# One inference step of a two-layer hybrid backbone on one core: out_proj's last token block is finished in the stage that follows

## What is computed

```python
h = rms_norm(x, g_pre1) * (1 + scale1) + shift1
y, ctx_out = token_mixers(h, *mix_params, ctx=ctx)
x = x + gate1 * rms_norm(y, g_post1)
h = rms_norm(x, g_pre2) * (1 + scale2) + shift2
x = x + gate2 * rms_norm(ffn(h), g_post2)
```

## Time and profile before

| | |
|---|---|
| median of three runs | 2105.94 us (2105.35 to 2110.06) |
| the profiled execution | 2105.66 us, span 2103.9 us |
| mean granted TensorE clock | 0.965 of full |
| PE busy | 1936.0 us, 92% of the span |
| DVE busy | 1296.7 us, 62% |
| ACT busy | 1046.1 us, 50% |
| POOL busy | 95.1 us, 5% |
| DMA | 302.25 MB, mean 144 GB/s, best of 40 slices 410 GB/s |
| loads `side<-ffn_w_gate`, issue to landing | 3.9 us, median |

### The profile page before, as it was taken

The page is one execution under the profiler, slowest core; times in us unless marked ns, Lnnn a source line. Parts: engine busy times, 40 slices in busy tenths (PEclk is TensorE's granted clock), DMA queues, the critical chain, the costliest instruction groups (busy, mean ns, idle before and its releaser), DMA issues. The chain is left out here.

```text
span 2103.9 us, 32195 instructions
## 1 busy us (share of the span) xinstructions
PE 1936.0 (92%) x11352; PEld 1618.4 (77%) x11352; DVE 1296.7 (62%) x1958; ACT 1046.1 (50%) x1689; POOL 95.1 (5%) x62
## 2 busy tenths in 40 slices
PE   4998899897999999997998999877999999999993
PEld 2996555597998998986986555876888888888883
DVE  3725656573323323356627565645888888888886
ACT  4214344444111112144235254535888888888884
POOL 0320000000000000001300000002000000000001
PEclk9999999898999999998999999888999999999997
DMA  6205512202223213212225601139967291827464
GB/s 252 95 26 200 198 41 101 100 1 71 76 81 96 70 63 90 80 41 90 70 81 213 266 1 40 62 136 393 410 250 282 87 345 50 343 94 275 173 245 160
DMA packets 130339, 302.25 MB, mean 144 GB/s; under 512 B 17984, under 2 KB 63936, under 8 KB 127296
## 3 DMA queue, kind: packets, MB, share of 16 engines
q1 hardware_dynamic: 124240, 279.10, 36.3%
q10 hardware_dynamic: 3120, 11.28, 1.4%
q0 software_dynamic: 2880, 10.49, 1.3%
HBM read 369.21 MB, written 28.61 MB: 189 GB/s over the span
## 5 line engine op out<-in xcount | busy, mean ns | idle before, releaser
L2208 DVE TENSOR_TENSOR ex_wl<-ex_raw,ex_wh 128x1024 fp32r<-128x1024 f32 x351 | 419.4, 1222 | 28.4 <-ACT ex_wh L2086 17.2
L2086 ACT ACTIVATE ex_wh<-ex_raw 128x1024 fp32r<-128x1024 f32 x351 | 368.2, 1060 | 74.7 <-PE psum L2143 46.2
L2491 PE MATMUL psum<-norm_out,ex_w_hi 128*128 128x320 f32 x1408 | 264.6, 309 | 4.3 <-PEq L1582 4.3
L2143 PE MATMUL psum<-ex_wh,ex_he_hi 128*128 128x512 f32 (+1 forms) x624 | 242.6, 389 | 12.7 <-DVE ex_wl L2208 12.7
L2143 PE MATMUL psum<-ex_wl,ex_he_hi 128*128 128x512 f32 (+1 forms) x624 | 233.5, 374 | 0.0
L2143 PE MATMUL psum<-ex_wh,ex_he_lo 128*128 128x512 f32 (+1 forms) x624 | 233.0, 373 | 0.0
L2491 PEld LDWEIGHTS psum<-norm_out,ex_w_hi 128*128 128x128 f32 x1408 | 222.2, 188 | 4.8 <-issue 4.6
L2358 DVE TENSOR_TENSOR ex_w_lo<-side,ex_w_hi 128x1024 fp32r<-128x1024 f32 (+1 forms) x82 | 82.6, 1014 | 169.4 <-ACT ex_w_hi L2354 169.2
L2491 PE MATMUL psum<-norm_out,ex_w_lo 128*128 128x320 f32 x704 | 160.3, 308 | 0.0
L2143 PEld LDWEIGHTS psum<-ex_wh,ex_he_hi 128*128 128x128 f32 x624 | 118.2, 189 | 35.3 <-issue 14.2
L2143 PEld LDWEIGHTS psum<-ex_wh,ex_he_lo 128*128 128x128 f32 x624 | 118.3, 190 | 22.0 <-issue 2.9
(11 more groups left out here) (401 smaller groups left out, 3819.9 us busy)
## 6 DMA issues: line engine op xcount, KB each, us to landing
ex_raw<-moe_gate_up SPq DMA_DIRECT2D x236, 512.0 KB
ex_raw<-moe_w_down SPq DMA_DIRECT2D x143, 512.0 KB
x<-moe_gate_up SPq DMA_DIRECT2D x70, 512.0 KB
wmod_ssd<-w_mod SPq DMA_DIRECT2D x56, 512.0 KB, 5.7
wmod_at<-w_mod SPq DMA_DIRECT2D x24, 512.0 KB, 4.2
side<-ffn_w_gate SPq DMA_DIRECT2D x22, 512.0 KB, 3.9
side<-ffn_w_up SPq DMA_DIRECT2D x22, 512.0 KB, 3.9
mx_qkv_room<-w_in SPq DMA_DIRECT2D x10, 1024.0 KB, 4.9
```

The source lines that it names most:

```text
L2086: act.activation(wh[:, i % RING], raw_of(i), ACT.Copy).then_inc(*hi_done.up(1))
L2143: last = pe.matmul(p.psum[:, 2 + g % 2, 0:width], h[:, k], w[:, i % RING, cols], start=(k == 0 and m == 0), stop=(k == KD - 1 and m == 2))
L2208: dve.tensor_tensor(wl[:, i % RING], raw_of(i), wh[:, i % RING].bitcast(F32), ALU.subtract).then_inc(*lo_done.up(1))
L2491: last = pe.matmul(p.psum[:, home[i] + half, 0:HT], m[:, slot, cols], x[:, k, half * HT:(half + 1) * HT], start=(k == 0 and n == 0), stop= ...
```

## The change

`stage_out_proj` ends with the products of block 4. The rest of block 4 goes into the next stage as two functions, `square_last` for ACT and `residual_last` for DVE, and the `Norm` object, whose counts are taken from the stage boundary (`closed`).

In `stage_dense` PE first makes the products of the first four pieces for the first half of the tokens (columns 0 to 319, blocks 0, 1 and half of 2), with the turn of block 4 ahead of the third, and then those of the second half. In `stage_router` the logits of blocks 0 to 3 and their two best are made apart from those of block 4. The order of row turns changes, all of them stand before the mask product, and the five pieces into x's room are issued first (four) and last (the fifth, after x of block 4 is stored). In the expert stage SP loads the first expert's last 13 pieces ahead of the loop, once `dispatched` is reached; the loop runs over the later passes, with the load of `xg` first in it; ACT takes the gathered tokens at once, and counts the early landings for the first pass. The table of block numbers shrinks, and the room of the dense low parts moves up. Cut below are the same edit in the other methods of `Norm`, the table, and the places of buffers.

```diff
         self.diagonal, self.scaled = diagonal, scaled
+        self.closed = 0
...
     def turn(self, pe, b, bank):
 
-        pe.wait_ge(*self.spread_out.at(b + 1))
+        pe.wait_ge(*self.spread_out.at(b + 1 - self.closed))
...
-                    for b in range(TB):
+                    for b in range(TB - 1):
...
-                for b in range(TB):
+                for b in range(TB - 1):
                     square(b, 0)
                     if b >= 1:
                         finish_norm(b - 1)
...
-                    if ahead and b == TB - 1:
-                        for i in range(2):
-                            act.wait_ge(ahead.landed[i], 16)
-                            ahead.high(act, i)
                     norm.statistics(act, b, res.at(b + 1))
                     norm.scale(act, b)
-                finish_norm(TB - 1)
+                square(TB - 1, 0)
+                finish_norm(TB - 2)
+                if ahead:
+                    for i in range(2):
+                        act.wait_ge(ahead.landed[i], 16)
+                        ahead.high(act, i)
...
-                pe.wait_ge(*norm.near.at(TB - 2))
-                pe.wait_ge(*norm.far.at(TB - 2))
-                norm.turn(pe, TB - 1, 2 * (TB % 2))
+                        if b == TB - 1 and i == 2:
+                            last.then_inc(*spent.up())
...
-                for b in range(TB):
-                    if b + 1 < TB:
-                        take_turned(b + 1)
+                for b in range(TB - 1):
+                    take_turned(b + 1)
                     if b == 0:
                         dve.wait_ge(*root.at(1))
                         dve.reciprocal(rstd[:, LB], rstd[:, LB]).then_inc(*rs.up())
                     else:
                         norm.take_near(dve, b - 1, 2 * (b % 2))
-                    take_residual(p, dve, link, b, p.psum[:, 4 + 2 * (b % 2):6 + 2 * (b % 2)], rows, upd,
-                                  stat2, rstd2, sq2, m2, r2, res)
+                    take_residual(p, dve, link, b, sums(b), rows, upd, stat2, rstd2, sq2.at(2 * b + 2), m2, r2.at(b + 1), res)
                     if b >= 1 and norm.split:
                         norm.keep_low(dve, b - 1)
                     norm.invert(dve, b)
+                norm.take_near(dve, TB - 2, 2 * ((TB - 1) % 2))
+                if norm.split:
+                    norm.keep_low(dve, TB - 2)
                 if ahead:
+                    dve.wait_ge(*spent.at(1))
                     for i in range(2):
                         dve.wait_ge(ahead.hi_done, i + 1)
                         ahead.low(dve, i)
-                norm.take_near(dve, TB - 1, 2 * (TB % 2))
-                if norm.split:
-                    norm.keep_low(dve, TB - 1)
     p.close_stage()
-
-
-def take_residual(p, dve, link, b, src, rows, upd, stat2, rstd2, sq2, m2, r2, res):
+    norm.closed = TB - 1
+    b = TB - 1
+
+    def square_last(act):
+
+        act.activation(used_up[:, 0:512], p.psum[:, 4 + 2 * (b % 2) + 1], ACT.Square,
+                       accum_out=stat2[:, b, 1:2]).then_inc(*sq2.up())
+        act.wait_ge(*m2.at(1))
+        act.activation(rstd2[:, b:b + 1], stat2[:, b, 0:1], ACT.Sqrt).then_inc(*r2.up())
+
+    def residual_last(dve, link):
+
+        take_residual(p, dve, link, b, sums(b), rows, upd, stat2, rstd2, sq2.at(1), m2, r2.at(1), res)
+    return norm, res, square_last, residual_last
...
-                sp.wait_ge(*p.sig("x_kept").at(0))
-                for i in range(EARLY):
+                sp.wait_ge(*x_kept.at(0))
+                for i in [*range(TB - 1), *range(TB, EARLY), TB - 1]:
+                    if i == TB + 3:
+                        sp.wait_ge(*x_done.at(1))
+                        sp.dma_start(r["kept_x"][(TB - 1) * P:TB * P], p.x[:, TB - 1]).then_inc(*x_kept.up(16))
+                    if i == TB - 1:
+                        sp.wait_ge(*x_kept.at(16))
+                        sp.wait_ge(*norm.spread_out.at(1))
...
-                for turn in range(2):
-                    for bank, (lo, hi) in enumerate(((0, 512), (512, T))):
+                def logits(bank, lo, hi):
+
+                    for turn in range(2):
...
-                last.then_inc(*lg_ps.up())
+                    return last
+
+                def turn_logits(b):
+
+                    return pe.transpose(p.psum[:, 2 + b // 4, (b % 4) * P:(b % 4 + 1) * P], rows[:, b * P:(b + 1) * P],
+                                        p.ident[:])
 
                 def turn_rows(b):
 
                     if b >= 2:
                         pe.wait_ge(*turned_act.at(b - 1))
...
+                logits(0, 0, 512).then_inc(*lg_ps.up())
                 turn_rows(0)
-                pe.wait_ge(*lg_rows.at(2))
-                for b in range(TB):
-                    last = pe.transpose(p.psum[:, 2 + b // 4, (b % 4) * P:(b % 4 + 1) * P], rows[:, b * P:(b + 1) * P],
-                                        p.ident[:])
+                pe.wait_ge(*lg_rows.at(1))
+                for b in range(LB):
+                    last = turn_logits(b)
                 last.then_inc(*lg_turned.up())
-                for b in range(1, 3):
+                norm.turn(pe, LB, 4)
+                pe.wait_ge(*norm.near.at(1))
+                pe.wait_ge(*norm.far.at(1))
+                logits(1, 512, T).then_inc(*rest_ps.up())
+                turn_rows(1)
+                pe.wait_ge(*rest_rows.at(1))
+                turn_logits(LB).then_inc(*lg_turned.up())
+                for b in range(2, TB):
                     turn_rows(b)
 
                 pe.wait_ge(*mask_ready.at(1))
...
-                for b in range(3, TB):
-                    turn_rows(b)
...
-                act.wait_ge(*lg_ps.at(1))
-                act.activation(rows[:, 512:T], p.psum[:, 1, 0:T - 512], ACT.Copy).then_inc(*lg_rows.up())
-                for b in range(TB):
+                def take_rows(b):
+
...
+                square_last(act)
+                norm.statistics(act, LB, x_done.at(1))
+                norm.scale(act, LB)
+                norm.take_far(act, LB, 4)
+                take_rows(0)
+                act.wait_ge(*rest_ps.at(1))
+                act.activation(rows[:, 512:T], p.psum[:, 1, 0:T - 512], ACT.Copy).then_inc(*rest_rows.up())
+                for b in range(1, TB):
+                    take_rows(b)
                 act.wait_ge(*best.at(1))
                 act.activation(e2[:], diff[:], ACT.Exp).then_inc(*e2_done.up())
 
...
+                residual_last(dve, link)
                 dve.wait_ge(*lg_ps.at(1))
                 dve.tensor_copy(rows[:, 0:512], p.psum[:, 0]).then_inc(*lg_rows.up())
+                norm.invert(dve, LB)
+
+                def two_best(b):
+                    link(dve, dve.max(top[:, b], lg[:, b]))
+                    link(dve, dve.max_index(idx[:, b], top[:, b], lg[:, b]))
                 dve.wait_ge(*lg_turned.at(1))
...
+                two_best(0)
+                two_best(1)
+                norm.take_near(dve, LB, 4)
+                two_best(2)
+                two_best(3)
+                dve.wait_ge(*lg_turned.at(2))
...
-                for b in range(TB):
-                    link(dve, dve.max(top[:, b], lg[:, b]))
-                    link(dve, dve.max_index(idx[:, b], top[:, b], lg[:, b]))
+                two_best(LB)
...
-                with sp.Fori(0, MAX_BLOCKS) as b:
-                    with sp.If(b < n):
-                        e = sp.value_load(r["table"][0:1, bass.ds(b, 1)], min_val=0, max_val=NE - 1)
-                        later, fresh = (sp.value_load(r["table"][0:1, bass.ds(b + n * MAX_BLOCKS, 1)], min_val=0, max_val=1)
-                                        for n in (1, 2))
-                        for i in range(N):
-
-                            if i < SPLIT:
-                                sp.wait_ge(*lo_done.at(b * SPLIT + i + 1))
-                            else:
-                                sp.wait_ge(*piece_done.at(b * N + i + 1))
-                            sp.dma_start(raw_of(i), expert_piece(io, e, i),
-                                         cond=later if i < EARLY else fresh).then_inc(*raw_in[LANDING_OF[i]].up(16))
-                        sp.wait_ge(r["dispatched"], 16 * 2 * TB)
+                others = sp.value_load(r["table"][0:1, 2 * MAX_BLOCKS + 1:2 * MAX_BLOCKS + 2], min_val=0, max_val=MAX_BLOCKS - 1)
+                sp.wait_ge(r["dispatched"], 16 * 2 * TB)
+                for i in range(EARLY, N):
+                    sp.dma_start(raw_of(i), expert_piece(io, 0, i)).then_inc(*raw_in[LANDING_OF[i]].up(16))
+                with sp.Fori(0, MAX_BLOCKS - 1) as b:
+                    with sp.If(b < others):
                         sp.wait_ge(*x_turned.at(b + 2))
                         sp.dma_start(xg[:], slot_rows((b + 2) * SL)).then_inc(*x_in.up(16))
+                        e = sp.value_load(r["table"][0:1, bass.ds(b + 1, 1)], min_val=0, max_val=NE - 1)
```

(73 more changed lines are left out.)

99 lines of the change are left out of this document (53 added, 46 removed).

## The result

| | before | after |
|---|---|---|
| median of runs, us | 2106.61 (5 runs, 2105.35 to 2110.06) | 2096.38 (5 runs, 2095.22 to 2097.55) |
| profiled execution: time, span | 2105.66, 2103.9 | 2096.19, 2094.4 |
| mean granted clock | 0.965 | 0.967 |

The ratio is 0.995, 95% interval 0.9938 to 0.9961: 10.2 us faster, where 12.1 had been predicted.

What follows compares the result with a forecast made beforehand. PE, busy 92% of the span, was taken as the bound, so only its idle or half-clock time could be won. Gains of 7.9 (layer 0) and 4.2 (layer 1) made 12.1, from 2105.66 to 2093.6 us; 2088.0 to 2099.5 for 8 in 10.

Steps and rivals of the forecast that it cites:

- both parts as summed: Whole kernel: layer 0's 7.9 and layer 1's 4.2 add up to 2093.6 us, own range 2090.5 to 2096.5; chance 0.50.
- Layer 0: Dense stage's opening: products start early and cover block 4's residual and turn; gain 7.9 us, between 6.2 and 9.5.
- The landing: Layer 0, SP's `high(2)` load: taken to land 5.5 us after issue, though the page's median for such loads is 3.9.
- Layer 1 to the gather: Router from PE's stop to the gather: gather starts 4.7 us earlier, net gain 3.3 after a clock charge.
- the mixed case: Layer 1 before the gather: clock falls, then returns during the row turns; gain 4.7, against 2.8 all cold and 7.3 all warm.
- The charge of 1.4 on the gather: Layer 1's gather: 1.4 us lost to half speed for some 3 us of its 9.2, after PE stands 2.9.
- The price drawn from it: Layer 1's gather, by the skill's rule on short bursts: gain only 2.8 less 1.7 us.
- The scatter: Layer 1, GpSimd: 18.9 us against 20.7, with two to four issues slowed by VectorE's splits; ends 5.1 us earlier.
- Late pieces: Layer 1's first expert: earlier start of PE gives nothing alone, only room for the scatter's gain, as piece 7 waits for it.
- First pass: Layer 1's first expert pass: piece 7 comes 5.1 us earlier, 0.9 charged for half clock, 4.2 remain.
- the rival of a late fetch: Later expert passes: each fetch starts late behind SP's xg load; at 1.5 us each the time is 2111.6; chance 0.03.

Runs made afterwards that it cites:

- split_late: The changed kernel with VectorE's first split made to wait until the whole scatter is over, a probe; 2103.22 us in one run.
- late_free: The changed kernel with SP's 13 late pieces issued at once beside the scatter, not behind it; 2108.3 us, ratio 1.0017 to the kernel before.
- l0_only: The kernel before with layer 0's part of the change alone, router and experts as before; 2097.58 us, ratio 0.9959 to the kernel before.
- wait11: The changed kernel with ScalarE's and VectorE's wait for the scatter moved from piece 7 to piece 11; 2089.16 us, ratio 0.9908 to the kernel before.
- pad15: The changed kernel with 15 idle products (2.2 us of PE work) in the dense stage ahead of the fifth piece; 2095.33 us, ratio 0.9941 to the kernel before.

## Why the prediction was right, by its steps

- **Which case.** The likeliest, both parts as summed: 2093.6 predicted, 2096.4 and 2095.0 measured, inside its own range and the 8-in-10 range, the first at the very edge of its own (2096.5).
- **Layer 0.** Start 3.9 after PE's stop, measured 3.79; residual's end 8.0 after it, measured 7.9 (488.40 + 1.23 - 481.77). The landing was taken at 5.5 and was 4.0, and the term was mis-sized by that: the turn was put 13.3 after the stop and came at 12.5, by then held by PE's own products. The first products did lose 1.6 to the half clock (the text's 1.7 is worked out from no row that it shows); the old wait would have ended at 492.19 + 1.15 + 0.3 = 493.6, so all but 0.6 of it hid there, as the text said it might. From the turn's start on 22.1 were predicted and 22.2 measured. 8.99 against 7.9.
- **Layer 1 to the gather.** Gain 4.7 predicted, 5.09 measured. The row turns bound the mask product, not the mask, as said: the mask was ready at 1404.3, the product ran at 1406.16. The clock fell near 1397 and was back near 1403.8, the mixed case taken. The charge of 1.4 on the gather was 1.6. 3.3 net predicted, 3.5 measured. The Trainium skill's rule on short bursts (TensorE: Matmul & The Clock Gate, "HAM oscillation — how this bites in real kernels") had named the danger: the clock did fall in both gaps. The price drawn from it did not come, a net gain of 1.1 against the 3.5 measured, because PE started the stage at full clock and had it back before the mask product.
- **The scatter.** 18.9 predicted, 18.96 measured, by a wrong mechanism, so that the number fits is luck. The issues under the splits took 1.76 to 1.97 (three, within the two to four said; the splits came 3.8 us into the scatter, where the text had 6, and the first product 38.8 after out_proj's end, where it had 40.5), but they cost nothing: `split_late` has them at 0.95 and lands at most 0.3 sooner. The slow issues speak against what the Trainium skill infers (SBUF — State Buffer, "Who interferes with whom") of descriptor writing. But an indirect issue also reads its row numbers (`slot`) from SBUF, which the same section's rule on two SBUF inputs would cover, and no run separates the two.
- **Late pieces.** Nothing of their own: 1.0004. What their waiting saves was taken too low: the text gave the scatter 1.8 for issues and landing together, while in `late_free` loads beside it made it 12 longer.
- **First pass.** Piece 7 5.23 earlier (5.1 predicted), the second pass 4.36 (4.2): 0.87 for the clock, 0.9 predicted. This is against the one profile of before; `l0_only` has the old code 2.22 faster there, so here too the close fit is in part luck.
- **Missing in the sum.** The 2.2 to 2.4 given back between the layers, and 0.05 in each of eleven passes. The sum took work that does not change at its old duration; the clock did not. With them 9.0 + 4.4 - 2.3 - 0.6 makes 10.5, against 12.1: layer 0 was put 1.1 too low and this 2.9 was left out, and the two errors partly cancel; the early start of the profile of before (1.4) and the tail (0.4) lead on to the 9.5 between the spans. The last 0.05 per pass (47.80 to 47.85) was not explained; the rival of a late fetch, which asked for 1.5 a pass, is refuted.
- **Not looked at.** The text took the wait before piece 7 as given; `wait11` won 7.3 us by it, more than any other single edit tried on the changed kernel.

## What to carry to other kernels

When a wait is taken away and its cause (here a scatter) still bounds the stage, look for the latest piece of work that truly needs it: moving one constant from 7 to 11 was worth 7 us, two thirds of what the whole rewrite gave. Keep bulk loads off the queues while a scatter that others wait for is under way (12 us here). And when stages behind the change open at half clock after a pause, count a shift of them as able to cost or give about 1 us at each such place, two of them here. Last, measure a stretch from a common event in each trace: starts in the span differed by up to 3.1 us between executions of the same code.

## What the hardware showed unexpectedly

- The delay between in_proj's start and the return of the full clock changed from 3.8 to 6.1 and back to 3.8 us (before, changed kernel, `pad15`) with equal work and equal pauses ahead of it. The clock was low for 17.1 us in all twelve profiles; only its fall lay elsewhere in the pause, 2.5 to 2.6 or 4.6 to 4.8 us after PE's stop.
- Ten scatters (5.2 MB by GpSimd) took 18.7 us with issues in 12.5, 19.0 with issues in 15.5, and 31 beside 13 loads of 512 KB by SP. In the first the DMA engines' busy share was 0.9 to 1.05 from 1422 to 1437, also behind the last issue.
- A GpSimd issue took 0.95 us with VectorE still, and 1.76 to 1.97 under its two-input splits.
- At the start of the dense stage 1.6 us were lost to half clock, of which only 0.6 showed, where a wait for another operand lay behind.
